# Chunked scan: a pair's first two transposed blocks moved ahead of the previous pair's output products

## The chip, the cores and the metric

The kernel runs on one core of a Trainium2 chip. Its time is the device time of one execution in microseconds (us); the time of a version is the median over its runs. The engines are TensorE (PE in the profile; PEld is its weight load), VectorE (DVE), ScalarE (ACT), GpSimd (POOL) and SyncE (SP), each with an instruction queue of its own. They meet only at semaphores.

## What is computed

The reference is a chain of transformer blocks on 512 tokens of 1024 channels in float32. What matters here is the recurrent layer in the first block: 12 heads of 64 channels, and for each head a state matrix that is carried over the tokens.

```python
def step(S, inp):
    r_t, w_t, k_t, v_t, a_t, b_t = inp
    sa = jnp.einsum('bhvk,bhk->bhv', S, a_t)
    S = (S * w_t[:, :, None, :] + sa[..., None] * b_t[:, :, None, :]
         + v_t[..., None] * k_t[:, :, None, :])
    return S, jnp.einsum('bhvk,bhk->bhv', S, r_t)
```

The kernel computes this in chunks of 64 tokens. Within a chunk the recurrence is a triangular system; its inverse is built by doubling, and what passes between chunks is folded in later.

## The kernel before

`scan_chunks` handles six pairs of heads (p = 0 to 5), two heads (e = 0, 1) side by side on the 128 partitions, four blocks of 128 tokens (q = 0 to 3), so eight chunks. Each engine runs its own list of steps in program order. `main_steps` names the steps of each engine in the order in which they count up its semaphore; `Steps.did` adds one at a step's end and `Steps.wait` waits for a named step of a pair, with `back=1` for the pair before. The order of `main_steps` and that of the code must be the same.

For one pair, TensorE does in this order:

- `b`: 16 products of bh with a and r, into the banks `bank_t`. They need the pair's ah and rh, and that the copy `wu1` of the pair before is done.
- `turn0`, `turn1`: eight transposes (four sources ah, bh, kh, v_still by two token blocks) into banks 6 and 7.
- `ab`: 16 products into `bank_x` (banks 0 and 1). The outputs of the pair before lie in banks 0, 1, 3 and 4, so it waits for ScalarE's `y` and VectorE's `q`.
- `k`: 16 products into `bank_m`, then `x0_1`, `x1_1`, then `turn2`, `turn3`.
- levels 1 to 5 of the inverse, products `x`, `m`, `t` for both e; `av` and the preparation's two sums of the next pair stand between them.
- `wu0`, `wu1`: 16 products; then, once ScalarE has copied both, `out`: 96 products that read the copied w|u, rb, aks and the tokens in `tok`.

ScalarE begins a pair with `square` (for the next pair), `tok0` (the copy of turn0 out of its bank), `ab0`, `ab1`, `tok1`, then the copies of x, `tok2`, `tok3` and more; it ends a pair with the copies `wu0`, `wu1`, and `h` and `y` of the outputs. VectorE begins with `inv_T` (mask of b's product), `inv_T_eye`, `rb`, `inv` (mask of ab), `aks` (mask of k), each for both e, then `decay_sum` of the next pair (L1006) and the additions of each level (`m` L1155, `t` L1159); it ends with `bonus` of the next pair, and `g` and `q` of the outputs (L1200, L1203). GpSimd cuts ab into level masks (`below`, L1219), adds the eye to inv (`inv_eye`, L1225), and makes the next pair's b, bh, kh (L1060) and rh (L1064).

While a pair's levels run, the other engines prepare the next pair: for pairs 0 to 4 all of ah, bh, kh, v_still and bonus of pair p + 1 are made before pair p's outputs end. TensorE's code is written out for all six pairs; the other engines loop.

All small products are recorded under the helper's line L1249, so the profile tells them apart by their operands: b is front_ar,front_bh, ab is front_bh,front_ar, k is front_ar,mixer_mixed. Transposes are L1259.

Of the kernel before, what the change touches and what calls it, by code (L numbers as in the profile page):

```python
# [19 lines left out]
ALU = mybir.AluOpType  # L20
# [301 lines left out]
MASK_LEVEL0_T, MASK_BEFORE_T, MASK_UPTO_T = 6, 7, 8  # L322
# [5 lines left out]

def main_steps():
    both = range(2)  # L330
    pe = ["b", "turn0", "turn1", "ab", "k", "x0_1", "x1_1", "turn2", "turn3", "m0_1", "t0_1", "m1_1"]
    for lv in range(2, 6):
        pe += [f"x0_{lv}", f"t1_{lv - 1}", f"x1_{lv}", f"m0_{lv}"] + ([f"t0_{lv}"] if lv < 5 else []) + [f"m1_{lv}"]
        pe += ["av"] if lv == 2 else []
    pe += ["wu0", "wu1", "out"]
    act = ["tok0", "ab0", "ab1", "tok1", "x0_1", "x1_1", "tok2", "tok3", "x0_2", "x1_2", "a_side", "x0_3", "av", "x1_3", "x0_4", "x1_4",
           "x0_5", "x1_5", "wu0", "wu1", "h", "y"]
    dve = [f"{n}{e}" for n in ("inv_T", "inv_T_eye", "rb", "inv", "aks") for e in both] + ["m0_1", "t0_1", "m1_1"]
    for lv in range(2, 6):
        dve += [f"t1_{lv - 1}", f"m0_{lv}"] + ([f"t0_{lv}"] if lv < 5 else []) + [f"m1_{lv}"]  # L340
    dve += ["g", "q"]
    pool = ["below1_0", "below1_1", "inv_eye0", "inv_eye1"] + [f"below{lv}_{e}" for lv in range(2, 6) for e in both]
    return act, dve, pool, pe
# [565 lines left out]
def scan_chunks(k, t, passes, mix):  # L909


    nc, ps, f, slab, lw, rate = k.nc, k.ps, t.f, t.slab, t.lw, t.rate
# [3 lines left out]
    rk_sum, kh = sq, kn  # L916
    bh, ar, ends = t.bh, t.ar, t.ends
    ah, rh = ar[:, 0, :], ar[:, 1, :]

    def two(name, shape):  # L920
        return [t.place(f"{name}{e}", [P, *shape]) for e in range(2)]

    inv_T, rb = (two(s, [TT, CH]) for s in ("inv_T", "rb"))
# [3 lines left out]
    ab, inv, x = (two(s, [TT, CH]) for s in ("ab", "inv", "x"))  # L927
# [4 lines left out]
    below, aks = two("below", [5, TT, CH]), two("aks", [TT, 2, CH])  # L932
    a_av, w_u = t.place("a_av", [P, 2, TT, P]), two("w_u", [TT, P])
    bank_x, bank_m, bank_t = ((e, e + 3) for e in range(3))
    act_s, dve_s, pool_s, pe_s = (Steps(f, n, s) for n, s in zip(
        ("act_done", "vector_done", "pool_done", "tensor_done"), main_steps()))
    act_p, dve_p, pool_p, pe_p = (Steps(f, n, s) for n, s in zip(
        ("act_prepared", "vector_prepared", "pool_prepared", "tensor_prepared"),
        (PREP_ACT, PREP_DVE, PREP_POOL, PREP_PE)))
# [11 lines left out]
    def on_tiles(mask):  # L951
        return mask.unsqueeze(1).broadcast_to([P, TT, CH])

    def mask(n):
        return on_tiles(k.tri[:, n, :])

    def low(bank):
        return ps[:, bank, 0:TT * CH].rearrange("p (q t) -> p q t", q=TT)

    def twos(bank):  # L960
        return ps[:, bank, :].rearrange("p (q w t) -> p q w t", q=TT, w=2)
# [15 lines left out]
    def still(act, p):  # L977
        pe_s.wait(act, "turn3", p, 1)
        dve_p.wait(act, "bonus", p, 1)
        act_p.did("v_still", act.copy(v_st[:], blk(slab, SLAB_V + p)))  # L980
# [106 lines left out]

    def begin_pe(pe):
        pe_s.begin(pe)
        pe_p.begin(pe)  # L1090

    def main(block, close):

        @block.scalar
        def _(act):
            def main(p, prep_next):
                def keep_tok(q):
                    pe_s.wait(act, f"turn{q}", p)
                    act_s.did(f"tok{q}", act.copy(tok[:, q, :, :], ps[:, 6 + q % 2, :].rearrange("p (n t) -> p n t", n=4)))

                def keep_x(e, lv):
                    pe_s.wait(act, f"x{e}_{lv}", p)
                    act_s.did(f"x{e}_{lv}", act.copy(x[e][:], low(bank_x[e])))

                if prep_next:
                    square(act, p + 1)
                keep_tok(0)
                for e in range(2):
                    pe_s.wait(act, "ab", p)
                    pool_s.wait(act, f"below5_{e}", p, 1)  # L1110
                    act_s.did(f"ab{e}", act.copy(ab[e][:], low(bank_x[e])))
                keep_tok(1)
                keep_x(0, 1)
                keep_x(1, 1)
                keep_tok(2)
                keep_tok(3)
                keep_x(0, 2)
                keep_x(1, 2)
                act_s.wait(act, "tok3", p)
                act_s.did("a_side", act.copy(a_av[:, :, :, 0:HD], tok[:, :, 0, :].rearrange("p q (e c) -> p e q c", e=2)))  # L1120
                if prep_next:
                    still(act, p + 1)
                else:
                    close.keep_memory(act)
                keep_x(0, 3)
                pe_s.wait(act, "av", p)
                act_s.did("av", act.copy(a_av[:, :, :, HD:P], ps[:, 6, :].rearrange("p (e q v) -> p e q v", e=2, q=TT)))
                keep_x(1, 3)
                keep_x(0, 4)
                if prep_next:  # L1130
                    root(act, p + 1)
                keep_x(1, 4)
                keep_x(0, 5)
                keep_x(1, 5)
                if prep_next:
                    decays(act, p + 1)
                for e in range(2):
                    pe_s.wait(act, f"wu{e}", p)
                    act_s.did(f"wu{e}", act.copy(w_u[e][:], ps[:, bank_t[e], :].rearrange("p (q c) -> p q c", q=TT)))
                pe_s.wait(act, "out", p)  # L1140
                act_s.did("h", act.copy(by_parity(blk(rate, p)), out_halves(*OUT_H)))
                act_s.did("y", act.copy(by_parity(blk(slab, SLAB_K + p)), out_halves(*OUT_Y)))

            with act.Fori(0, PAIRS - 1) as p:
                main(p, True)
            main(PAIRS - 1, False)
            close.act(act)

        @block.vector
        def _(dve):  # L1150
            def main(p, prep_next):
# [13 lines left out]
                    dve_s.wait(dve, f"inv_T{e}", p)  # L1165
                    dve_s.did(f"inv_T_eye{e}", dve.tensor_tensor(inv_T[e][:], inv_T[e][:], on_tiles(k.eye64[:]), ALU.add))
                for e in range(2):
                    dve_s.did(f"rb{e}", dve.tensor_tensor(rb[e][:], twos(bank_t[e])[:, :, 1, :], mask(MASK_UPTO_T), ALU.mult))
                for e in range(2):
                    act_s.wait(dve, f"ab{e}", p)  # L1170
                    dve_s.did(f"inv{e}", dve.tensor_tensor(inv[e][:], ab[e][:], mask(0), ALU.mult))
                for e in range(2):
                    pe_s.wait(dve, "k", p)
                    dve_s.did(f"aks{e}", dve.tensor_tensor(aks[e][:], twos(bank_m[e]), k.tri[:, MASK_BEFORE_T:MASK_UPTO_T + 1, :].unsqueeze(1)
                                                           .broadcast_to([P, TT, 2, CH]), ALU.mult))
# [71 lines left out]
        def _(pe):  # L1247
# [8 lines left out]
            def main(p, prep_next):  # L1256
                def turn(q):
                    for n, src in enumerate((ah, bh, kh, v_st)):
                        last = pe.transpose(ps[:, 6 + q % 2, n * P:(n + 1) * P], src[:, q * P:(q + 1) * P], k.ident[:])  # L1259
                    pe_s.did(f"turn{q}", last)  # L1260

                def make_x(e, lv):
                    pool_s.wait(pe, f"below{lv}_{e}", p)
# [33 lines left out]
                for q in range(TT):  # L1297
                    for e, rows, c, cs in quads:
                        last = mm(ps[cs, bank_t[e], q * P:(q + 1) * P], bh[rows, chunk(q, c)], ar[rows, :, chunk(q, c)])
                pe_s.did("b", last)  # L1300
                if p == 0:
                    t.banks_free(pe, 1)
                act_p.wait(pe, "v_still", p)
                dve_p.wait(pe, "bonus", p)
                act_s.wait(pe, "av", p, 1)
                turn(0)
                turn(1)
                act_s.wait(pe, "y", p, 1)
                dve_s.wait(pe, "q", p, 1)
                for q in range(TT):  # L1310
                    for e, rows, c, cs in quads:
                        last = mm(ps[cs, bank_x[e], q * CH:(q + 1) * CH], ah[rows, chunk(q, c)], bh[rows, chunk(q, c)])
                pe_s.did("ab", last)
                if p == 0:
                    t.banks_free(pe, 0)
                for q in range(TT):
                    for e, rows, c, cs in quads:
                        last = mm(ps[cs, bank_m[e], q * P:(q + 1) * P], kh[rows, chunk(q, c)], ar[rows, :, chunk(q, c)])
# [12 lines left out]
                for lv in range(2, 6):  # L1331
# [7 lines left out]
                    if lv == 2:  # L1339
                        act_s.wait(pe, "tok3", p)  # L1340
                        for e in range(2):
                            for q in range(TT):
                                at = (e * TT + q) * HD
                                for cs in halves:
                                    last = mm(ps[cs, 6, at:at + HD], aks[e][cs, q, 0, :], tok[cs, q, 3, halves[e]])
# [5 lines left out]
                for e in range(2):  # L1351
                    act_s.wait(pe, "av", p)
                    dve_s.wait(pe, f"m{e}_5", p)
                    for q in range(TT):
                        for cs in halves:
                            last = mm(ps[cs, bank_t[e], q * P:(q + 1) * P], inv_T[e][cs, q, :], a_av[cs, e, q, :])
                    pe_s.did(f"wu{e}", last)
                act_s.wait(pe, "wu0", p)
                act_s.wait(pe, "wu1", p)
                w, u = slice(0, HD), slice(HD, P)  # L1360
                for q in range(TT):
# [11 lines left out]
                    for e, rows, c, cs in quads:  # L1373
                        last = mm(ps[rows, 3 + c, hi], tok[cs, q, 2, rows], tok[cs, q, 3, rows], start=False)
# [3274 lines left out]
```

## Time and profile before

| | |
|---|---|
| median of 3 runs | 1821.3 us (1820.88 to 1821.97) |
| the profiled execution's own time | 1820.98 us |
| its span in the profile | 1819.3 us |
| TensorE busy in the span | 1772.5 us (97%) |
| VectorE, ScalarE, GpSimd busy | 69%, 52%, 18% |
| the scan's stretch in the profile | about 188 to 370 us |
| page slices of TensorE in tenths, 40 slices | 8999888899999999999999999999999999999998 |

The profile records one execution. Times in its timeline are us from the span's start. A row of the timeline merges operations of one kind: start, length, engine, line, operation, output<-inputs, shape and count; the brackets give the idle time of the engine before the row and what ended it. "issue" there is idle time in which the engine waited for nothing that the profile shows. Merged rows of two engines' operations can overlap, since an operation's length holds its start-up and its last write.

### The profile page before, as it was taken

The numbers are of one execution on the slowest core, as the hardware profiler recorded it, in microseconds if no ns is written. First come the engines' busy times: TensorE is split into PE (matmuls) and PEld (weight loads), VectorE is DVE, ScalarE is ACT, GpSimd is POOL, SyncE is SP. The second block draws the span as 40 slices with busy tenths as digits, with TensorE's granted clock in tenths as the row PEclk, the third lists the DMA queues.
The fourth block names the chain that finished last, engine by engine and source line by source line (L and its number), as shares of the span: only waits on it lengthen the run. The fifth ranks groups of instructions, "written<-read, shape, count | busy, mean of one in ns | idle before, by whom it ended". The sixth has DMA issues, their size and how long they took to land. (4 is left out here: it accounts for less than half of the span.)

```text
span 1819.3 us, 37312 instructions
## 1 busy us (share of the span) xinstructions
PE 1772.5 (97%) x15389; PEld 1543.6 (85%) x15389; DVE 1249.6 (69%) x1913; ACT 946.4 (52%) x1670; POOL 321.8 (18%) x359
## 2 busy tenths in 40 slices
PE   8999888899999999999999999999999999999998
PEld 6777777868988999878896698999998989999997
DVE  5346766657866676567568668777777887777776
ACT  6633444446644444345479656544445865544454
POOL 3012576724300000000034104000005040000000
PEclk9999999999999999999999999999999999999999
DMA  5222000003222233372200122333333213333331
GB/s 196 93 70 70 26 4 4 28 9 92 95 93 93 93 111 99 99 141 93 87 8 2 54 86 70 105 105 105 105 115 118 71 35 105 105 105 105 99 103 66
DMA packets 152252, 148.27 MB, mean 82 GB/s; under 512 B 13692, under 2 KB 150042, under 8 KB 152090
## 3 DMA queue, kind: packets, MB, share of 16 engines
q1 hardware_dynamic: 151964, 145.91, 26.0%
q8 instruction: 122, 2.00, 0.5%
q14 instruction: 40, 0.33, 0.1%
q10 hardware_dynamic: 126, 0.04, 0.0%
HBM read 143.84 MB, written 2.10 MB: 80 GB/s over the span
## 5 line engine op out<-in xcount | busy, mean ns | idle before, releaser
L1851 DVE TENSOR_TENSOR weight_low<-weight_ring,weight_high 128x1024 fp32r<-128x1024 f32 (+2 forms) x250 | 254.0, 1024 | 147.9 <-ACT weight_high L1839 147.7
L1839 ACT CAST weight_high<-weight_ring 128x1024 fp32r<-128x1024 f32 (+2 forms) x250 | 215.2, 865 | 247.0 <-PE psum L248 116.1
L1886 PE MATMUL psum<-tail_x_high,weight_high 128*128 128x256 f32 x1008 | 282.8, 281 | 1.0 <-DVE weight_low L1851 0.6
L1887 PE MATMUL psum<-tail_x_low,weight_high 128*128 128x256 f32 x1008 | 282.4, 280 | 0.0
L1888 PE MATMUL psum<-tail_x_high,weight_low 128*128 128x256 f32 x1008 | 282.3, 280 | 0.0
L1886 PEld LDWEIGHTS psum<-tail_x_high,weight_high 128*128 128x128 f32 x1008 | 189.7, 188 | 3.4 <-DVE weight_low L1851 0.9
L1887 PEld LDWEIGHTS psum<-tail_x_low,weight_high 128*128 128x128 f32 x1008 | 189.7, 188 | 1.6
L1888 PEld LDWEIGHTS psum<-tail_x_high,weight_low 128*128 128x128 f32 x1008 | 189.7, 188 | 0.0
L246 PE MATMUL psum<-tail_hidden_high,weight_high 128*128 128x512 f32 (+1 forms) x400 | 147.8, 370 | 0.0
L248 PE MATMUL psum<-tail_hidden_high,weight_low 128*128 128x512 f32 (+1 forms) x400 | 147.5, 369 | 0.0
L247 PE MATMUL psum<-tail_hidden_low,weight_high 128*128 128x512 f32 (+1 forms) x400 | 147.4, 368 | 0.0
L228 DVE TENSOR_TENSOR weight_low<-weight_ring,weight_high 128x2048 fp32r<-128x2048 f32 (+1 forms) x32 | 72.5, 2264 | 98.7 <-ACT weight_high L219 98.6
L1886 PE MATMUL psum<-middle_x,weight_high 128*128 128x256 f32 x392 | 110.3, 281 | 0.0
L1887 PE MATMUL psum<-middle_x,weight_high 128*128 128x256 f32 x392 | 109.9, 280 | 0.0
L1888 PE MATMUL psum<-middle_x,weight_low 128*128 128x256 f32 x392 | 109.9, 280 | 0.0
L1958 ACT COPY tail_quads<-psum 128x256 f32<-128x256 f32 x144 | 53.7, 373 | 101.4 <-PE psum L1888 100.4
L248 PEld LDWEIGHTS psum<-tail_hidden_high,weight_low 128*128 128x128 f32 x400 | 75.4, 188 | 13.9
L246 PEld LDWEIGHTS psum<-tail_hidden_high,weight_high 128*128 128x128 f32 x400 | 75.4, 189 | 13.0 <-DVE tail_hidden_low L4048 0.5
L219 ACT CAST weight_high<-weight_ring 128x2048 fp32r<-128x2048 f32 (+1 forms) x32 | 59.7, 1867 | 50.6 <-PE psum L248 42.5
L247 PEld LDWEIGHTS psum<-tail_hidden_low,weight_high 128*128 128x128 f32 x400 | 75.4, 188 | 12.5
L1839 ACT CAST weight_high<-tail_sums 128x1024 fp32r<-128x1024 f32 x72 | 60.2, 836 | 35.3 <-DVE tail_sums L1806 29.5
L1886 PEld LDWEIGHTS psum<-middle_x,weight_high 128*128 128x128 f32 x392 | 73.9, 188 | 0.8 <-issue 0.2
(559 smaller groups left out, 4756.0 us busy)
## 6 DMA issues: line engine op xcount, KB each, us to landing
weight_ring<-in_w_ff SPq DMA_DIRECT2D x32, 1024.0 KB, 5.3
weight_ring<-in_ffn_w_gate SPq DMA_DIRECT2D x22, 1024.0 KB, 5.4
weight_ring<-in_ffn_w_up SPq DMA_DIRECT2D x22, 1024.0 KB, 5.4
weight_ring<-in_ffn_w_down SPq DMA_DIRECT2D x32, 512.0 KB, 4.6
weight_ring<-in_rw_in SPq DMA_DIRECT2D x10, 1024.0 KB, 5.4
weight_ring<-in_attn_w_in SPq DMA_DIRECT2D x9, 1024.0 KB, 5.2
weight_ring<-in_ffn_w_down SPq DMA_DIRECT2D x8, 768.0 KB, 4.7
weight_ring<-in_w_out SPq DMA_DIRECT2D x4, 1024.0 KB, 5.1
```

Of the source, the lines that this page charges most:

```text
L219: act.copy(self.w_hi[:, slot, 0:n], self.ring[:, slot, 0:n]).then_inc(self.panel_high, 1)
L228: dve.tensor_tensor(self.w_lo[:, slot, 0:n], self.ring[:, slot, 0:n], self.w_hi[:, slot, 0:n], ALU.subtract).then_inc(self.panel_low, 1)
L246: pe.matmul(out, w_hi, x_hi, start=start, stop=False)
L247: pe.matmul(out, w_hi, x_lo, start=False, stop=False)
L248: return pe.matmul(out, w_lo, x_hi, start=False, stop=stop)
L1839: last = act.copy(high, source)
L1851: last = dve.tensor_tensor(low, source, high, ALU.subtract)
L1886: pe.matmul(out, w_hi, x_hi, start=kk == 0 and not more, stop=False, skip_group_check=more)
L1887: pe.matmul(out, w_hi, x_lo, start=False, stop=False, skip_group_check=more)
L1888: last = pe.matmul(out, w_lo, x_hi, start=False, stop=kk == kp - 1, skip_group_check=more)
L1958: act.copy(to, self.bank(pos, 2 if n == 1 else 0)).then_inc(self.kept, 1)
```

## The change

TensorE's `turn0` and `turn1` of pair p + 1 are issued in pair p, behind `wu1` and ahead of `out`, with all their waits (now for ah, kh and `tok3` too). For pair 0 they stand behind `ab`. They count on a semaphore of their own, `first_tiles_turned`. In a pair, `ab` then follows `b` directly. ScalarE copies `tok1` directly behind `tok0`, ahead of `ab0`. VectorE masks `inv` ahead of `rb`. No operation is added or taken away, and no DMA is moved.

```diff
-    pe = ["b", "turn0", "turn1", "ab", "k", "x0_1", "x1_1", "turn2", "turn3", "m0_1", "t0_1", "m1_1"]
+    pe = ["b", "ab", "k", "x0_1", "x1_1", "turn2", "turn3", "m0_1", "t0_1", "m1_1"]
...
-    act = ["tok0", "ab0", "ab1", "tok1", "x0_1", "x1_1", "tok2", "tok3", "x0_2", "x1_2", "a_side", "x0_3", "av", "x1_3", "x0_4", "x1_4",
+    act = ["tok0", "tok1", "ab0", "ab1", "x0_1", "x1_1", "tok2", "tok3", "x0_2", "x1_2", "a_side", "x0_3", "av", "x1_3", "x0_4", "x1_4",
...
-    dve = [f"{n}{e}" for n in ("inv_T", "inv_T_eye", "rb", "inv", "aks") for e in both] + ["m0_1", "t0_1", "m1_1"]
+    dve = [f"{n}{e}" for n in ("inv_T", "inv_T_eye", "inv", "rb", "aks") for e in both] + ["m0_1", "t0_1", "m1_1"]
...
+    pe_t = Steps(f, "first_tiles_turned", ["turn0", "turn1"])
...
                 keep_tok(0)
+                keep_tok(1)
                 for e in range(2):
                     pe_s.wait(act, "ab", p)
                     pool_s.wait(act, f"below5_{e}", p, 1)
                     act_s.did(f"ab{e}", act.copy(ab[e][:], low(bank_x[e])))
-                keep_tok(1)
...
                 for e in range(2):
-                    dve_s.did(f"rb{e}", dve.tensor_tensor(rb[e][:], twos(bank_t[e])[:, :, 1, :], mask(MASK_UPTO_T), ALU.mult))
-                for e in range(2):
                     act_s.wait(dve, f"ab{e}", p)
                     dve_s.did(f"inv{e}", dve.tensor_tensor(inv[e][:], ab[e][:], mask(0), ALU.mult))
+                for e in range(2):
+                    dve_s.did(f"rb{e}", dve.tensor_tensor(rb[e][:], twos(bank_t[e])[:, :, 1, :], mask(MASK_UPTO_T), ALU.mult))
...
+                def first_turns(p):
+                    act_p.wait(pe, "v_still", p)
+                    dve_p.wait(pe, "ah", p)
+                    pool_p.wait(pe, "kh", p)
+                    dve_p.wait(pe, "bonus", p)
+                    act_s.wait(pe, "av", p, 1)
+                    act_s.wait(pe, "tok3", p, 1)
+                    turn(0)
+                    turn(1)
...
-                act_p.wait(pe, "v_still", p)
-                dve_p.wait(pe, "bonus", p)
-                act_s.wait(pe, "av", p, 1)
-                turn(0)
-                turn(1)
                 act_s.wait(pe, "y", p, 1)
                 dve_s.wait(pe, "q", p, 1)
...
                 pe_s.did("ab", last)
+                if p == 0:
+                    first_turns(0)
                 if p == 0:
                     t.banks_free(pe, 0)
...
                     pe_s.did(f"wu{e}", last)
+                if prep_next:
+                    first_turns(p + 1)
                 act_s.wait(pe, "wu0", p)
                 act_s.wait(pe, "wu1", p)
```

## Rows read from the trace of the kernel before

**Rows 1.** Timeline, pair 0: kh on GpSimd, second w|u copy, outputs' first weight load.

```profile
212.24 1.72 POOL L1060 TENSOR_TENSOR mixer_mixed<-mixer_mixed 128x512 f32<-128x512 f32 x1
...
213.89 0.59 ACT L1139 COPY scan_w_u<-psum 128x512 f32<-128x512 f32 x1 [0.29 <-PE psum L1249]
...
214.59 0.35 PEld L1249 LDWEIGHTS psum<-scan_rb,scan_w_u 64*64 64x64 f32 x16 [0.99 <-ACT scan_w_u L1139]
```

**Rows 2.** Timeline, pair 0 to 1: outputs' restart, then b, turns, ab, level 1.

```profile
218.35 0.25 PEld L1249 LDWEIGHTS psum<-scan_rb,scan_w_u 64*64 64x64 f32 x10 [1.44 <-issue]
...
219.42 0.59 ACT L1141 COPY rwkv_lw_rate<-psum 128x512 f32 x1 [4.94 <-PE psum L1249]
...
220.04 0.68 DVE L1203 TENSOR_TENSOR rwkv_slab<-psum,rwkv_slab 128x512 f32 x1
220.07 0.14 PEld L1259 LDWEIGHTS psum<-identity,front_ar 128*128 128x128 f32 x1 [0.17 <-issue]
...
220.64 0.74 DVE L1163 TENSOR_TENSOR scan_inv_T<-psum,first_block_chunk_masks 128x256 f32<-128x256 f32 x2
...
221.00 0.58 ACT L1099 COPY scan_tok<-psum 128x512 f32<-128x512 f32 x1
221.09 0.56 PEld L1249 LDWEIGHTS psum<-front_bh,front_ar 64*64 64x64 f32 x32 [0.17 <-issue]
...
221.94 0.65 ACT L1111 COPY scan_ab<-psum 128x256 f32<-128x256 f32 x2 [0.35 <-PE psum L1249]
221.97 0.74 DVE L1168 TENSOR_TENSOR scan_rb<-psum,first_block_chunk_masks 128x256 f32<-128x256 f32 x2
222.39 1.59 POOL L1219 TENSOR_TENSOR scan_below<-scan_ab,first_block_chunk_masks 128x256 f32<-128x256 f32 x2 [7.21 <-ACT scan_ab L1111]
...
222.63 1.63 DVE L1171 TENSOR_TENSOR scan_inv<-scan_ab,first_block_chunk_masks 128x256 f32<-128x256 f32 x2
...
225.38 1.25 DVE L1006 TENSOR_TENSOR_SCAN mixer_mixed<-first_block_restart,rwkv_lw_rate 128x512 f32<-128x512 f32 x1
...
225.67 0.54 PEld L1249 LDWEIGHTS psum<-scan_x,scan_inv 64*64 64x64 f32 x16 [0.17 <-DVE scan_aks L1174]
...
226.56 0.39 DVE L1155 TENSOR_TENSOR scan_inv_T<-psum,scan_inv_T 128x256 f32<-128x256 f32 x1
...
227.21 0.55 PEld L1249 LDWEIGHTS psum<-scan_inv_T,scan_below 64*64 64x64 f32 x16
```

**Rows 3.** Timeline, pair 1 to 2: q, restart inside b, masks, first addition.

```profile
249.37 0.68 DVE L1203 TENSOR_TENSOR rwkv_slab<-psum,rwkv_slab 128x512 f32 x1
...
250.09 0.42 PEld L1249 LDWEIGHTS psum<-front_ar,front_bh 64*64 64x64 f32 x15 [1.24 <-issue]
...
250.81 0.76 DVE L1163 TENSOR_TENSOR scan_inv_T<-psum,first_block_chunk_masks 128x256 f32<-128x256 f32 x2 [0.76 <-PE psum L1249]
...
252.55 0.65 ACT L1111 COPY scan_ab<-psum 128x256 f32<-128x256 f32 x2 [0.59 <-PE psum L1249]
252.96 1.29 DVE L1171 TENSOR_TENSOR scan_inv<-scan_ab,first_block_chunk_masks 128x256 f32<-128x256 f32 x2
253.00 1.83 POOL L1219 TENSOR_TENSOR scan_below<-scan_ab,first_block_chunk_masks 128x256 f32<-128x256 f32 x2 [6.93 <-ACT scan_ab L1111]
...
257.33 0.42 DVE L1155 TENSOR_TENSOR scan_inv_T<-psum,scan_inv_T 128x256 f32<-128x256 f32 x1 [0.73 <-PE psum L1249]
```

**Rows 4.** Windows from restart to restart: length, then busy us and count per engine.

```profile
218.34:250.08 31.74, 28.17 (x881) 24.82 (x881) 22.20 (x41) 15.16 (x33) 20.51 (x22) 1.00 0.01 4
250.08:279.99 29.91, 25.69 (x754) 22.52 (x754) 19.55 (x37) 12.60 (x28) 20.56 (x22) 1.00 0.01 3
```

**Rows 5.** DMA view of 215.5 to 217.2 us: throughput in 40 slices, packets.

```profile
GB/s 0 0 0 386 0 0 0 0 0 0 0 0 0 0 0 0 0 0 0 0 0 0 0 0 0 0 0 0 0 0 0 0 0 0 0 0 0 0 0 0
...
q8 instruction: 1, 0.02, 4.6%
```

**Rows 6.** Timeline, start of pair 0: copies of turn0 and of ab.

```profile
189.64 0.59 ACT L1099 COPY scan_tok<-psum 128x512 f32<-128x512 f32 x1 [0.41 <-PE psum L1259]
...
190.81 0.65 ACT L1111 COPY scan_ab<-psum 128x256 f32<-128x256 f32 x2 [0.59 <-PE psum L1249]
```

More of the change, by code:

```diff
@@ L1089, in begin_pe @@
         pe_s.begin(pe)
+        pe_t.begin(pe)
         pe_p.begin(pe)
@@ L1097, in keep_tok @@
                 def keep_tok(q):
-                    pe_s.wait(act, f"turn{q}", p)
+                    (pe_t if q < 2 else pe_s).wait(act, f"turn{q}", p)
                     act_s.did(f"tok{q}", act.copy(tok[:, q, :, :], ps[:, 6 + q % 2, :].rearrange("p (n t) -> p n t", n=4)))
@@ L1259, in turn @@
                         last = pe.transpose(ps[:, 6 + q % 2, n * P:(n + 1) * P], src[:, q * P:(q + 1) * P], k.ident[:])
-                    pe_s.did(f"turn{q}", last)
+                    (pe_t if q < 2 else pe_s).did(f"turn{q}", last)
+                def first_turns(p):
[7 more added lines that the diff above has]
+                    turn(1)
                 def make_x(e, lv):
```

## The prediction

> **What bounds the kernel now.** The page shows TensorE busy nearly throughout, but that is an average: in the scan, the only stage that the change touches, work passes from engine to engine. So I read the timeline of the places where one pair of heads hands over to the next. There are five: T0 (pair 0 to 1) to T4. T2 repeats T0 and T3 repeats T1; T4 has no preparation work behind it; pair 0's own start is a sixth place.
>
> In T0, TensorE waits 0.99 us for the second copy of w|u before the output products [rows 1]. It runs them from 214.59, stops, and goes on at 218.35 after 1.44 us in which no engine keeps it waiting [rows 2]. Then come b, eight transposes (turn0, turn1), and ab at 221.09. Meanwhile VectorE reads the outputs (g, q) and does inv_T, its eye, rb, inv, aks and the decay sum back to back, from q at 220.04 to 226.63, and its next operation, the addition of m0_1, begins at 226.56 in the profile's overlapping figures. TensorE starts x0_2 at 227.21, only 0.26 after that addition's end at 226.95 [rows 2]. So from the outputs' end to the second level T0 is bound by VectorE, and TensorE, with turns in it, is barely behind. That is the thing to see: the transposes stand in TensorE's queue, but not on a path of their own.
>
> In T1 the stop falls later, into b: b goes on at 250.09 after 1.24 us, when q has already ended (250.05). Here VectorE waits 0.76 us for b, and the addition of m0_1 waits 0.73 us for TensorE: T1 is bound by TensorE up to that addition [rows 3].
>
> What is the stop? TensorE issued 881+881 instructions from the restart in T0 to that in T1, and 754+754 from there to the next: a difference of 254 [rows 4]. In the 1.7 us around T0's stop, one packet of 0.02 MB moves on the instruction queue, in the fourth of 40 slices from 215.5, so at about 215.6 [rows 5]; the restart comes 2.7 us behind it. I read the stops as code arriving in pieces of some 256 instructions: dense stretches of small matmuls use one piece up before the next is there. The Trainium skill, "Runtime: NRT & Kernel Launch", section "Instruction fetch mechanics", also has pieces of 256 instructions, but calls the cost of crossing into one mostly hidden. Here it is not hidden. If it were, the delay of the outputs worked out below would pass on in full, and the sum would be 2.3 us instead of 1.1.
>
> **The change, part by part.**
>
> *Turns ahead of the outputs.* They need kh of the next pair, which GpSimd ends at 212.24+1.72 = 213.96 [rows 1]. With 0.1 us for the news to travel (214.59 less the end of w|u's copy at 214.48), they start at 214.07. The eight take 221.09-220.07 = 1.02 us with the change-over behind them [rows 2], so the outputs start at 215.09 instead of 214.59: 0.5 us late. The 0.99 us hole takes only half of the block. Does the 0.5 reach the outputs' end? The outputs still need the next piece of code. It is asked for once the sequencer is past its wait for w|u at 214.5, in either order, so it arrives at 218.35 as before and the late start eats 0.5 of the 1.44 us. The 16 instructions moved ahead, and about three for waits, push the piece's edge 19 instructions earlier; at ab's rate (64 in 0.56 us [rows 2]) that leaves 0.15 us more to do after the restart. T0: outputs end 0.15 late; bounds 0 and 0.5.
>
> *ab directly behind b.* ab must still wait until q has read its bank. q ends at 220.72 now [rows 2], 220.87 then; ab starts at 220.98 instead of 221.09. Of 1.02 us taken out, 0.1 is gained, because q was next.
>
> *tok1 ahead of ab0 on ScalarE.* ScalarE goes h, y, square, tok0 without a hole: four starts from 219.42 to 221.00, durations 0.59, 0.59, 0.73, so each overlaps the next by 0.1 and a tok copy (0.58) costs 0.48. Then tok0 starts at 221.15, tok1 at 221.63, ab0 at 222.11, against 221.94 now, when it waited 0.35 us for ab [rows 2]. So ab0 comes 0.17 later, not earlier. Behind it wait GpSimd's cuts, VectorE's inv, and through the cuts x0_1.
>
> *inv ahead of rb.* rb filled VectorE's time until ab0. Now VectorE ends the eye at 222.05+0.15 = 222.20, idles until ab0's copy is there (222.5), and rb's 222.63-221.97 = 0.66 us comes after. inv starts at 222.5 instead of 222.63 and everything from aks on is 0.66-0.13 = 0.53 later. What inv-first is to feed, GpSimd's inv_eye, stands behind both cuts, which occupy GpSimd until 222.39+1.59 = 223.98 [rows 2]: an earlier inv is of no use there. inv pays by contention: its two operations took 1.63 us in T0, where the cut started 0.24 earlier, and 1.29 in T1, where both started within 0.04, with the cuts at 1.83 instead of 1.59 [rows 2, 3]. The new order makes every place like T1: VectorE gains up to 0.34 back (0.53 becomes 0.2), and TensorE's x1_1, turn2, turn3 and m0_1 come 0.17+0.24 = 0.41 later. The Trainium skill, "SBUF — State Buffer", section "SBUF: two separate sides", says that the two engines share a port pair which the first holds for its whole instruction while the other fully blocks. By it a cut that starts last would cost its full wait, some 0.4 us (such an operation takes 0.39 at 226.56 [rows 2]), instead of the 0.24 shown, and T0 would be 0.15 us dearer.
>
> **T0:** the addition of m0_1 is late by 0.2 to 0.55 us, and TensorE by 0.41; TensorE has only 0.2 us of room at x0_2. I take +0.4. T2 is the same: +0.4.
>
> **T1:** the outputs start 0.5 late and end 0.5 late, since their stop comes only in b: q ends at 250.55. The next piece is asked for from inside the running outputs, so 0.5 less 0.14 later: b goes on at 250.45 with about 19 instructions more, ends about 0.6 late, and VectorE's inv_T starts at 251.4 instead of 250.81. ab follows at once, its copy at 251.95 instead of 252.55 [rows 3]: TensorE gains 0.6 up to m0_1. VectorE does not: inv_T, eye, inv, rb, aks, decay sum take 226.63-220.64 = 6.0 us in T0 [rows 2], so they end at 257.3, and the addition of m0_1 stays at 257.3 (257.33 now). T1: -0.1, with -0.5 as the bound if inv runs at its fast rate beside an early cut. T3 the same.
>
> **T4:** ScalarE has no square before tok0 and VectorE no decay sum, which would give up to 0.4 us; but the edges have by then crept so far that the piece after the stop may end inside ab. I take +0.2, bounds -0.4 and +0.6.
>
> **Pair 0:** here ab goes ahead of the turns, and ScalarE copies tok0 and tok1 before ab0. tok0 starts at 189.64 now; with ab's 0.5 us ahead of its turns it starts at about 190.15, tok1 at 190.63, ab0 at 191.1, against 190.81 [rows 6]. +0.3, bounds 0 and +0.7.
>
> **Sum:** 0.3 + 0.4 - 0.1 + 0.4 - 0.1 + 0.2 = **+1.1 us**. The profiled execution took 1820.98 us, its span 1819.3, 0.3 below the median of 1821.3; everything after the scan starts that much later, and the page's slices show TensorE nine tenths busy or more nearly all the way from there, so nothing takes it up. 1820.98+1.1 = 1822.1, or on the median 1822.4. A change below 0.2% (3.6 us) I count as none, which is about what a measurement of this kernel tells apart.
>
> **The rivals.**
> *It pays as drawn.* If what counts were TensorE's own queue, each of the five handovers would lose the 1.02 us block: 5.1 us, 1816.2. For it: the 0.99 us hole exists, and in T1 TensorE is the bound. Against: in T0, VectorE's unbroken 6 us, none of which the change removes. Chance 0.09.
> *The masks' new order costs in full.* VectorE is the line; rb's 0.66 us falls behind inv in six places without the 0.34 of contention returned, and ab0 is no earlier: 6 x 0.66 = 4.0 us, 1825.3. It decides where ab0's copy comes 0.66 us or more behind the eye. For it: ScalarE delivers ab0 later. Against: I find 0.3 in T0, and in T1 it comes before the eye. With the delay of the outputs passing too it could reach 1827. Chance 0.17.
> *Nothing moves.* Code arrival fixes the outputs' end and T1 and T3 return what T0 and T2 lose: 1821.3. Chance 0.24.
> The forecast itself: 0.50.
>
> **How the numbers follow.** Faster 0.09, same 0.50+0.24 = 0.74, slower 0.17. With all lower bounds (0, +0.2, -0.5, +0.2, -0.5, -0.4) the time is 1820.3, with the upper ones (0.7, 0.55+0.35 unabsorbed, 0, the same, 0, 0.6) 1824.4. Widened towards the rivals: 1819.8 to 1825.6.
>
> **What the changed profile would show.** Right, if: turns begin about 0.1 us behind kh's end and the outputs about 0.5 late; T0's restart stays 3.8 us behind the outputs' old start; ab begins within 0.2 us of q's end; ScalarE has no idle time ahead of ab0; VectorE idles some 0.3 us before inv in T0, and its inv pair takes 1.3 us with cuts at 1.8. Wrong, if the outputs' end moves by 0.5 or not at all, if code stops fall inside ab or ahead of w|u, or if the preparation's kh is later than the w|u products.

## The result and the profile after

The changed kernel takes 1823.78 us (median, 1822.82 to 1824.82) against 1821.41 of the kernel before measured beside it: ratio 1.0013, interval 1.0007 to 1.0019, so 2.4 us more (1.3 to 3.5). A second measurement gave 1.0014 (1.0005 to 1.0023). The change costs a little, less than the 0.2% that I had set as the bound. The span of the profiled execution is 1821.4 us, 2.1 more. The forecast was +1.1, so the measured loss is twice as large, and the time lies within the range; but two of its terms, those of T3 and T4, were wrong, and in the profiled execution they are most of what the scan lost.

T0 in the timeline of the changed kernel; these rows answer to [rows 1] and [rows 2] (lines have moved by one to four):

```profile
212.68 1.72 POOL L1061 TENSOR_TENSOR mixer_mixed<-mixer_mixed 128x512 f32<-128x512 f32 x1
...
214.57 0.14 PEld L1261 LDWEIGHTS psum<-identity,front_ar 128*128 128x128 f32 x1 [0.53 <-issue]
...
215.60 0.32 PEld L1251 LDWEIGHTS psum<-scan_rb,scan_w_u 64*64 64x64 f32 x16 [0.17 <-issue]
...
218.75 0.14 PEld L1251 LDWEIGHTS psum<-scan_tok 64*64 64x64 f32 x3 [0.98 <-issue]
...
220.57 0.68 DVE L1205 TENSOR_TENSOR rwkv_slab<-psum,rwkv_slab 128x512 f32 x1
...
221.37 0.59 PEld L1251 LDWEIGHTS psum<-front_bh,front_ar 64*64 64x64 f32 x32 [0.94 <-ACT rwkv_slab L1144]
221.54 1.07 ACT L1101 COPY scan_tok<-psum 128x512 f32<-128x512 f32 x2
...
222.48 0.68 ACT L1114 COPY scan_ab<-psum 128x256 f32<-128x256 f32 x2
...
222.92 1.29 DVE L1171 TENSOR_TENSOR scan_inv<-scan_ab,first_block_chunk_masks 128x256 f32<-128x256 f32 x2 [0.33 <-ACT scan_ab L1114]
222.96 1.83 POOL L1221 TENSOR_TENSOR scan_below<-scan_ab,first_block_chunk_masks 128x256 f32<-128x256 f32 x2 [7.33 <-ACT scan_ab L1114]
...
224.13 0.74 DVE L1173 TENSOR_TENSOR scan_rb<-psum,first_block_chunk_masks 128x256 f32<-128x256 f32 x2
...
227.30 0.42 DVE L1157 TENSOR_TENSOR scan_inv_T<-psum,scan_inv_T 128x256 f32<-128x256 f32 x1
...
227.88 0.55 PEld L1251 LDWEIGHTS psum<-scan_inv_T,scan_below 64*64 64x64 f32 x16
```

The reader is to measure from kh's end, 214.40 here and 213.96 before, so that earlier shifts drop out. The outputs start 1.20 us behind it instead of 0.63, yet q starts 6.17 behind it instead of 6.08: the stop, 0.98 instead of 1.44 us, has taken up nearly all of the delay. ab starts 0.12 us behind the end of q (221.25): TensorE's own queue no longer holds it, q does, and from kh it starts 6.97 us on, 0.16 earlier than before, which this kernel doesn't use: ScalarE is still copying tok1. From there the delay grows again: ab0 8.08 instead of 7.98, VectorE idle for 0.33 ahead of inv, the cuts at 1.83. x0_2 starts 13.48 us behind kh instead of 13.25.

T3 and T4 look different. T3 of the kernel before restarts inside b, as T1 does [rows 3]:

```profile
311.55 0.52 PEld L1249 LDWEIGHTS psum<-front_ar,front_bh 64*64 64x64 f32 x18 [1.05 <-issue]
```

T3 of the changed kernel:

```profile
312.32 0.13 PEld L1251 LDWEIGHTS psum<-scan_tok 64*64 64x64 f32 x1 [1.16 <-issue]
...
313.35 0.68 DVE L1205 TENSOR_TENSOR rwkv_slab<-psum,rwkv_slab 128x512 f32 x1
...
313.95 0.75 DVE L1165 TENSOR_TENSOR scan_inv_T<-psum,first_block_chunk_masks 128x256 f32<-128x256 f32 x2
```

And T4, the first ab products, a second stop, the last ones, and the copy that waits for them:

```profile
345.54 0.54 PEld L1251 LDWEIGHTS psum<-front_bh,front_ar 64*64 64x64 f32 x27 [0.94 <-ACT rwkv_slab L1144]
...
346.31 0.14 PEld L1251 LDWEIGHTS psum<-front_bh,front_ar 64*64 64x64 f32 x3 [0.23 <-issue]
...
346.69 0.65 ACT L1114 COPY scan_ab<-psum 128x256 f32<-128x256 f32 x2 [0.52 <-PE psum L1251]
```

In T3 the first instruction behind the stop is still one of the outputs (`scan_tok`), not one of b (`front_ar,front_bh`) as before. So the whole stop of 1.16 us stands ahead of the outputs' last product, and g, q and h wait it out: q starts 6.27 us behind kh's end instead of 4.53. In T4 the edge of the piece after that lies inside ab; the stop there is 0.23 us.

The ledger: start of x0_2 less the end of kh (for pair 0 less the start of b), each from two such rows, in us:

| | pair 0 | T0 | T1 | T2 | T3 | T4 | sum |
|---|---|---|---|---|---|---|---|
| before | 8.37 | 13.25 | 13.06 | 13.37 | 13.03 | 13.21 | 74.3 |
| changed | 8.53 | 13.48 | 12.87 | 13.35 | 13.57 | 13.86 | 75.7 |
| difference | +0.16 | +0.23 | -0.19 | -0.02 | +0.54 | +0.65 | +1.4 |
| forecast | +0.3 | +0.4 | -0.1 | +0.4 | -0.1 | +0.2 | +1.1 |

T3 and T4 carry 1.2 of the 1.4 us. A ledger comes from one execution: the same kernel profiled twice gave sums of 75.7 and 76.1, and another pair (the candidate below) 72.1 and 73.1, with the stops of unequal length (in T4 of the changed kernel 1.27 and 1.54 us). Where the stops fall was the same in both profiles of each pair. Single cells therefore count from about 0.5 us on, and times of eleven runs tell apart about 1.6 us.

### The profile page after: what moved, and what is told of

The parts are those of the page before. It is cut to its first block and busy times, and to the rows that moved or that the text cites. A ratio compares the mean times of both kernels' runs of the same rounds, so it can differ in the third digit from the quotient of the medians.

```text
span 1821.4 us, 37325 instructions
## 1 busy us (share of the span) xinstructions
PE 1773.2 (97%) x15389; PEld 1544.6 (85%) x15389; DVE 1249.3 (69%) x1913; ACT 945.6 (52%) x1670; POOL 322.8 (18%) x359
```

## The experiments

There are twelve runs, ten kernels and two repeats, in three sets, each set on one chip; all ratios are to the kernel before in the same set. Where a run is compared with the changed kernel of another set, the comparison goes through the kernel before.

**One part alone, and the changed kernel with fewer waits.**

*masks_only:*

```diff
 # the kernel before
+                for e in range(2):
+                    act_s.wait(dve, f"ab{e}", p)
+                    dve_s.did(f"inv{e}", ...)
                 for e in range(2):
                     dve_s.did(f"rb{e}", ...)
-                for e in range(2):
-                    act_s.wait(dve, f"ab{e}", p)
-                    dve_s.did(f"inv{e}", ...)
```

> The kernel before with one part of the change: VectorE masks inv ahead of rb. Nothing of TensorE's code is touched. Theory (code edges): the change's loss sits where TensorE's stop for code falls, so this part costs little: in T0, T2, T4 and pair 0 the cuts on GpSimd take 0.96 instead of 0.72 us because inv starts with them, some 0.2 us each; in T1 and T3 the additions waited 0.73 us for TensorE and hide rb's 0.66. Sum +0.9 us. Rival (masks cost in full): 0.66 us in each of six places, +4.0 us. Second rival (inv-first feeds GpSimd): faster by some 0.3 us a place, -1.8 us.

Measured: 1822.17 against 1820.44 us, ratio 1.0008 (0.9999 to 1.0017), so +1.5 (-0.2 to +3.1), +1.7 by the medians. The full price of 4.0 us and the second rival's gain of 1.8 are outside the interval; no cost at all is not. Its ledger is 0.5 us more than before, with T3 at 13.20 and T4 at 13.18. T0 in its timeline, with TensorE's code untouched:

```profile
221.98 0.65 ACT L1111 COPY scan_ab<-psum 128x256 f32<-128x256 f32 x2 [0.35 <-PE psum L1249]
222.39 1.29 DVE L1169 TENSOR_TENSOR scan_inv<-scan_ab,first_block_chunk_masks 128x256 f32<-128x256 f32 x2 [0.29 <-ACT scan_ab L1111]
222.43 1.83 POOL L1219 TENSOR_TENSOR scan_below<-scan_ab,first_block_chunk_masks 128x256 f32<-128x256 f32 x2 [6.93 <-ACT scan_ab L1111]
223.60 0.74 DVE L1171 TENSOR_TENSOR scan_rb<-psum,first_block_chunk_masks 128x256 f32<-128x256 f32 x2
```

The masks' order alone turns T0's pair 1.63 and 1.59 [rows 2] into 1.29 and 1.83, and opens a hole of 0.29 us on VectorE.

*copies_only:*

```diff
 # the kernel before
                 keep_tok(0)
+                keep_tok(1)
                 for e in range(2):
                     ...  # ab0, ab1
-                keep_tok(1)
```

> The kernel before with one part of the change: ScalarE copies tok1 directly behind tok0, ahead of ab0. TensorE still does the turns between b and ab, so tok1 fills the time in which ScalarE waits 0.35 to 0.59 us for ab. Theory: 0 to +0.3 us in all. Rival (ScalarE's order sets the pace): a copy of 0.48 us ahead of ab0 in six places, up to +2.9 us.

Measured: 1820.69, ratio 1.0000 (0.9991 to 1.0009). As expected, no cost that can be measured; the rival's 2.9 us is outside the interval.

*turns_only:*

```diff
 # the changed kernel
-                keep_tok(1)
                 for e in range(2):
                     ...  # ab0, ab1
+                keep_tok(1)
...
+                # rb again ahead of inv on VectorE
```

> The changed kernel with ScalarE's and VectorE's orders of before; TensorE's list is that of the changed kernel, instruction for instruction. Theory (code edges): the stops in T3 (inside the last two outputs) and T4 (inside ab) stay, so most of the loss stays: +1.2 to +1.8 us against before, T3's x0_2 later by about 0.5 us against its kh and T4's by about 0.5. Rival (masks and copies cause the loss): 0 us or less, and T3 and T4 like T1 and T2.

Measured: 1821.23, ratio 1.0003 (0.9994 to 1.0012): +0.8 by the medians, below what I had expected, and the interval holds both theories. The ledger tells more: pair 0 is 8.34, as before, and T0 to T2 are 12.99, 12.79, 12.98, each 0.3 to 0.4 better than before; T3 13.50 and T4 14.59 are the two bad ones, though neither masks nor copies are changed. The stops lie where they lie in the changed kernel, the late one of T4 now 0.78 us long:

```profile
310.64 0.13 PEld L1251 LDWEIGHTS psum<-scan_tok 64*64 64x64 f32 x1 [1.44 <-issue]
...
345.11 0.14 PEld L1251 LDWEIGHTS psum<-front_bh,front_ar 64*64 64x64 f32 x3 [0.78 <-issue]
```

So T3 and T4 lose without those two parts.

*three_waits:*

```diff
 # the changed kernel
                 def first_turns(p):
-                    act_p.wait(pe, "v_still", p)
-                    dve_p.wait(pe, "ah", p)
                     pool_p.wait(pe, "kh", p)
                     dve_p.wait(pe, "bonus", p)
                     act_s.wait(pe, "av", p, 1)
-                    act_s.wait(pe, "tok3", p, 1)
```

> The changed kernel with three of the six waits ahead of the moved turns left out because the others imply them (bonus comes after ah and v_still, av after tok3). The work and its order are the same; TensorE's code is two instructions shorter for each pair, so each code edge comes later in the stream. Theory (code edges): in T3 the stop leaves the outputs and falls into b, in T4 the second edge leaves ab and falls into k. T3 gains about 0.7 us and T4 0.4: +1.2 us against before instead of +2.4. Rival (the loss is work on a path): no difference that can be measured against the changed kernel, +2.3 us, and T3 unchanged.

Measured: 1821.73, ratio 1.0008 (0.9999 to 1.0017): +1.3 by the medians. The stop in T3 went where it was expected, into b:

```profile
309.73 0.69 DVE L1202 TENSOR_TENSOR rwkv_lw_rate<-psum,first_block_eye 128x512 f32 x1 [2.25 <-PE psum L1251]
310.34 0.68 DVE L1205 TENSOR_TENSOR rwkv_slab<-psum,rwkv_slab 128x512 f32 x1
311.11 0.74 PEld L1251 LDWEIGHTS psum<-front_ar,front_bh 64*64 64x64 f32 x26 [1.60 <-issue]
...
312.25 0.76 DVE L1165 TENSOR_TENSOR scan_inv_T<-psum,first_block_chunk_masks 128x256 f32<-128x256 f32 x2 [1.24 <-PE psum L1251]
```

g and q now run during the stop. But in this execution the stop lasted 1.60 us and inv_T waited 1.24 for b, so T3's ledger is 13.46, hardly better than 13.57; T4's is 13.02 instead of 13.86, and T1's 12.22 instead of 12.87. The four later profiles with three waits have T3's stop in b too, and there T3 is 12.86, 12.85, 12.59 and 12.90, T4 12.77 to 13.07; the three with six waits have T3 at 13.57, 13.57 and 13.50, T4 at 13.86 to 14.59. On these profiles' means T3 gains about 0.6 us by the edge in b, of which the waits' own time can be 0.1. There is a second, smaller gain that I had not expected. T0 ahead of the outputs:

```profile
211.84 1.72 POOL L1061 TENSOR_TENSOR mixer_mixed<-mixer_mixed 128x512 f32<-128x512 f32 x1
...
213.61 0.14 PEld L1261 LDWEIGHTS psum<-identity,front_ar 128*128 128x128 f32 x1 [0.41 <-POOL mixer_mixed L1061]
```

The transposes start 0.05 us behind kh's end, with six waits 0.17: in the changed kernel three waits are still to be worked off when kh is there.

**The edges moved on purpose, the hole filled twice, and the candidate.**

*after_24_longer* and *before_24_longer:*

```diff
 # the changed kernel, and the kernel before
+    filler = f.sem("filler")
...
                 if p == 0:
                     t.banks_free(pe, 2)
+                    for _ in range(24):
+                        pe.sem_inc(filler, 1)
```

> The changed kernel with 24 instructions put into TensorE's stream ahead of pair 0's b (each adds one to a semaphore that nobody waits for; TensorE's sequencer is there 3.6 us ahead of the products still running, so their own 1.2 us are covered). No work of the scan is changed, only where the code's edges fall: 24 instructions earlier. Theory (code edges): T1's stop, now in b's first products, falls into the outputs as T3's does (+0.6 us), and in T0 and T2 the second edge leaves k and falls into ab (+0.6 us each); +1.8 us against the changed kernel, +4.2 against before. Rival (edges don't matter): no difference from the changed kernel, +2.4 against before.

> The kernel before with the same 24 instructions. Theory: here the turns stand between b and ab, both late stops stay inside b (395 and 385 instructions into a block whose outputs end at 384), and the second edges fall at the end of ab, at 528, 518 and 508: 0 to 0.5 us in all. Rival (the 24 instructions themselves cost): +1.2 us, and the same in the changed kernel.

Measured: 1824.44 against 1820.88, ratio 1.0020 (1.0011 to 1.0029), +3.6; and 1821.61, ratio 1.0007 (0.9998 to 1.0016). So some +1.2 on the changed kernel and +0.7 on the one before. The intervals alone don't separate these; T1 of the first does:

```profile
251.73 0.20 PEld L1252 LDWEIGHTS psum<-scan_tok 64*64 64x64 f32 x5 [1.45 <-issue]
252.23 0.69 DVE L1203 TENSOR_TENSOR rwkv_lw_rate<-psum,first_block_eye 128x512 f32 x1 [3.98 <-PE psum L1252]
252.84 0.68 DVE L1206 TENSOR_TENSOR rwkv_slab<-psum,rwkv_slab 128x512 f32 x1
```

T1's stop has left b for the outputs, and T1 is 13.92 us, with the scan's work unchanged, against 12.87 and 13.15 in the two profiles of the changed kernel: one place, +0.8 to +1.05. The half of the theory about ab came out weaker: T0 13.54 and T2 13.40 against 13.48 and 13.35, since the next piece had nearly arrived (stops of 0.3 and 0.1 us inside ab). In the kernel before, both odd stops stayed in b.

*twice_turned:*

```diff
 # the changed kernel
                     act_s.wait(pe, "tok3", p, 1)
+                    for q in range(2):
+                        for n, src in enumerate((ah, bh, kh, v_st)):
+                            pe.transpose(ps[:, 6 + q % 2, n * P:(n + 1) * P], src[:, q * P:(q + 1) * P], k.ident[:])
                     turn(0)
                     turn(1)
```

> The changed kernel with turn0 and turn1 done twice in succession, 0.9 us more of transposes ahead of the outputs in every handover. Theory (the stop absorbs): in T0 the outputs start 0.9 us later against kh and end only 0.1 to 0.2 later, the 1.1 us stop shrinks to 0.2 or 0.3; in T1 and T3, whose stop lies at the outputs' end, the delay passes. Some +3.5 to +4 us against the changed kernel, most of it in T1, T3 and pair 0. Rival (no absorption): the outputs' end in T0 is 0.9 us later against kh, and +5.4 us in all.

Measured: 1827.79 against 1820.88, ratio 1.0037 (1.0023 to 1.0050): +6.7 (4.2 to 9.1), some 4.4 over the changed kernel. T0:

```profile
213.42 1.72 POOL L1061 TENSOR_TENSOR mixer_mixed<-mixer_mixed 128x512 f32<-128x512 f32 x1
...
217.21 0.32 PEld L1251 LDWEIGHTS psum<-scan_rb,scan_w_u 64*64 64x64 f32 x16 [0.17 <-issue]
...
219.70 0.14 PEld L1251 LDWEIGHTS psum<-scan_tok,scan_w_u 64*64 64x64 f32 x3 [0.56 <-issue]
...
221.76 0.68 DVE L1205 TENSOR_TENSOR rwkv_slab<-psum,rwkv_slab 128x512 f32 x1
```

From kh's end (215.14) the outputs start at 2.07, 0.87 later than in the changed kernel, and q at 6.62, 0.45 later: half is absorbed, not nine tenths. The restart comes 4.56 behind kh instead of 4.35, and more outputs stand behind it, since the doubled block puts the edge 32 instructions earlier. In T2 and T4 the outputs run without a stop: in T4 the additional instructions have pushed it on into b, and in T2, where the edge ahead of it falls before the transposes, the packet starts 2.8 us before the outputs do and no stop is seen. There q comes earlier than in the changed kernel (5.89 instead of 6.05 and 6.45) and the ledger is 13.19 and 13.23 instead of 13.35 and 13.86, in spite of 0.87 us more of transposes. That is the strongest evidence that the stop, by its place or by its absence, outweighs the block.

*turns_three_waits* (the candidate):

```diff
 # the changed kernel
 # first_turns with the waits for kh, bonus and av alone, as in three_waits
 # ScalarE: tok0, ab0, ab1, tok1; VectorE: rb ahead of inv, both as before
```

> The candidate: turns moved with three waits only, ScalarE's and VectorE's orders as before the change. Theory: the edges are those of three_waits (T3's stop in b, T4's second edge in k), the masks' order costs nothing any more: -0.5 to +0.5 us against before, so no difference that can be measured, and some 1.5 us faster than the changed kernel. Rival (the moved turns pay once the other two parts are gone): -3 us or more.

Measured: 1819.57 against 1820.88, ratio 0.9993 (0.9984 to 1.0002). Ledger: 8.37, 12.83, 12.37, 12.92, 12.86, 12.77, sum 72.1 against 74.3.

**The candidate, and the two orders put back one at a time.**

*changed_repeat* is the changed kernel, *three_repeat* the candidate, word for word; no edit.

> The changed kernel again, so that it stands beside the next three on one chip: +2.4 us against before.

> The candidate again (turns moved with three waits, ScalarE's and VectorE's orders of before): -1.3 us against before as in its first run if that was real, 0 if it was chance. Against the changed kernel beside it: -3.5 us.

*rb_first_three* and *inv_first_three:*

```diff
 # the candidate: ScalarE's order changed (rb_first_three)
                 keep_tok(0)
+                keep_tok(1)
...
 # the candidate: VectorE's order changed (inv_first_three)
+                # inv ahead of rb
```

> The candidate with ScalarE's new order (tok1 ahead of ab0), rb still ahead of inv. TensorE's code is the candidate's, instruction for instruction. Theory (the masks' order is the costly one, by GpSimd's cuts at 0.96 instead of 0.72 us and rb behind inv on VectorE): -1 us against before, within 0.5 of the candidate. Rival (ScalarE's order costs): +1 us against before.

> The candidate with VectorE's new order (inv ahead of rb), ScalarE's as before. Theory: this carries most of the 2.2 us between the candidate and three_waits: +0.5 to +1 us against before. Rival (ScalarE's order costs): -1 us, like the candidate.

| third set | median us | to before | ratio (interval) |
|---|---|---|---|
| before | 1820.99 | | |
| changed_repeat | 1823.53 | +2.5 | 1.0014 (1.0005 to 1.0023) |
| inv_first_three | 1821.53 | +0.5 | 1.0003 (0.9994 to 1.0012) |
| rb_first_three | 1820.56 | -0.4 | 0.9998 (0.9988 to 1.0007) |
| three_repeat | 1819.70 | -1.3 | 0.9994 (0.9985 to 1.0003) |

The candidate lies 3.8 us below the changed kernel (the two intervals don't meet) and 1.3 below the kernel before in both sets, where each interval still takes in 1: a small gain is likely and not shown. By medians inv-first costs 1.8 us on top of the candidate and tok1-first 0.9, less than their intervals. T3 of the candidate, in its first profile, shows what rb-first leaves: VectorE goes from the eye to rb without a hole.

```profile
311.57 0.74 PEld L1251 LDWEIGHTS psum<-front_ar,front_bh 64*64 64x64 f32 x26 [1.40 <-issue]
...
313.38 0.75 DVE L1168 TENSOR_TENSOR scan_inv_T<-scan_inv_T,first_block_eye 128x256 f32<-128x256 f32 x2
...
314.05 0.75 DVE L1170 TENSOR_TENSOR scan_rb<-psum,first_block_chunk_masks 128x256 f32<-128x256 f32 x2
```

## Why the prediction was right, and where not

- **VectorE sets T0's pace, so taking the turns from between b and ab earns next to nothing there.** ab starts right behind q, and in the changed kernel x0_2 comes no earlier. Without the other two parts it comes a little earlier (T0 12.99 in turns_only, 12.83 and 13.25 in the candidate, 13.25 before), but inv begins 8.66 us behind kh in turns_only and 8.67 before: what is gained is a shorter overlap of inv with the cuts, not the 1.02 us block. The rival's 5.1 us lies outside the interval of every run.
- **Turns start 0.1 us behind kh, outputs 0.5 late.** 0.17 and 0.57. The difference is waits that TensorE works off one by one behind kh; three_waits starts at 0.05.
- **The stop absorbs the delay of the outputs (0.15 left).** In T0 q is 0.09 late for 0.57: right. The packet on the instruction queue starts 1.70 us behind kh's end before, 1.66 in the changed kernel and 1.65 in twice_turned, while the outputs start at 0.63, 1.20 and 2.07: the piece is asked for at the same time in all three, as assumed. Doubled, only half was absorbed: the rule holds while the stop is long enough and its edge stays put. That stops mark pieces of 256 instructions is borne out by where they fell: in all kernels the distance between the handovers' restarts was a multiple of 256, waits included, and an edge moved by the number of instructions put in or taken out, to within one (23 for the 24, 2 for each set of waits shortened up to there). What issues the pieces was not looked into further. The Trainium skill's "mostly hidden" ("Runtime: NRT & Kernel Launch", "Instruction fetch mechanics") is contradicted by stops of 0.9 to 1.6 us in every handover.
- **tok1-first delays ab0 by 0.17.** In T0 0.10 from kh against before, and 0.36 against turns_only, where ab0 follows tok0. With ab late anyway no cost is seen (copies_only 1.0000); with ab early there may be one (0.9 us by medians, unresolved).
- **inv-first: a hole of 0.3 us, inv 1.29, cuts 1.83.** 0.33, 1.29 and 1.83, so the dearer T0 of a full block did not come. Price +1.7 us alone and 1.8 on the candidate, by medians, neither clear of its interval; the rival's 4.0 is outside masks_only's.
- **Pair 0 and T0.** Forecast +0.3 and +0.4, ledger +0.16 and +0.23: right in direction.
- **T1.** Forecast -0.1, ledger -0.19, and +0.09 in the second profile: right. q came 0.49 late and ab's copy 0.79 early, which VectorE, without a hole now, could not use. b's restart, forecast 0.36 late, was not late (5.12 us behind kh's end, 5.25 before).
- **T2.** Forecast +0.4, ledger -0.02: too dear. Its restart came sooner in this execution (4.12 us behind kh's end, 4.35 in T0).
- **T3. The step that failed: "T3 the same".** I had worked out that the edge moves 19 instructions earlier and creeps from pair to pair, used that for T4, and did not apply it to T3. From the outputs' first instruction, of 384, the stop lay at 419 (T1) and 409 (T3) before, and lies at 396 and 382 now: 382 is two instructions inside the outputs. The forecast's 19 alone would have left it at 390, six behind them: the waits took five instructions in the first place instead of three, and two more in each place after it, 27 by T3. This is +0.54 instead of -0.1. after_24_longer did the same to T1 on purpose, and it took 0.8 to 1.05.
- **T4. The term was mis-sized:** the place (the second edge inside ab) was right, the size 0.65 instead of 0.2. That stop is 0.23 us, and q comes 0.18 later; ab's copy is then 0.32 late, and the other 0.33 is added behind it. The size varies: 13.86 and 14.13 in the changed kernel's two profiles, 14.59 in turns_only. A stop inside ab was one of the prediction's own signs of being wrong.
- **Sum.** Terms that erred down by 1.1 (T3, T4) and up by 0.7 (pair 0, T0, T2) partly cancel; that the time fell into the range owes something to this, and is in part luck. One sum of the prediction does not come out: if the stop took up nothing, its terms give 0.35 us more in T0 and in T2, so 1.8 us, or 2.15 with T4 as well, not 2.3. The ledger's 1.4, 0.26 us by which this profile's scan starts later, and some 0.4 in the later levels and close make the 2.1 us of the spans.

Shown: the candidate against the changed kernel, 3.8 us, so the three waits and the two orders together carry the loss. Open: how much of the 2.4 us is each part's. The medians give moved turns with three waits -1.3, three more waits +1.1, inv-first +1.8, tok1-first +0.9, which add up to 2.5, but each has an error of over 1 us, and the waits' 1.1 cannot be split between the edges that they move and their own time. Why a piece of code arrives at times 0.4 us later was not tried.

## What to carry to other kernels

Where an engine issues hundreds of small instructions in a row, count them: a stop for code of about 1 us, as in every handover here, can stand in the stream, and whether it stands ahead of or behind the instruction that others wait for is decided by a handful of instructions, waits among them. A moved block is paid for by the engine that is the line there, not by the queue that it leaves: look first which engine has no hole between the two points. And a wait that another implies is not free: here three of them took 0.12 us a place.

## What was not expected of the hardware

- A stop in code supply takes up a delay put in front of it: 0.57 us of later start left 0.09 at the outputs' end; 0.87 us more left 0.45.
- 24 instructions that do nothing for the result made T1 0.8 to 1.05 us longer by moving a stop across the last output product.
- Six waits instead of three put 0.12 us between kh and the first transpose, in five places.
